# A two-layer encoder on eight cores: the first layer's gates fed from un-normed x, with the norm's factor multiplied onto the sums

## The reference, cut to what matters

```python
def rms_norm(x, g):
    y = xf * lax.rsqrt(jnp.mean(xf * xf, axis=-1, keepdims=True) + EPS)
    return (y * g.astype(jnp.float32)).astype(x.dtype)

# layer 0; x: (2, 8192, 1024)
h = rms_norm(x, norm_0)
z = h @ w_in_0                       # a_u, a_v, a_gate, b_x, b_gate, 1024 columns each
ya = spatial_gating_mixer(a_u, a_v, ...) * jax.nn.silu(a_gate)
yb = multiscale_pool_mixer(b_x, b_group_w_0, b_scale_0) * jax.nn.silu(b_gate)
x = x + jnp.concatenate([ya, yb], axis=-1) @ w_out_0
# layer 1: rms_norm, q/k/v/gate projection, windowed attention, output projection, residual
return rms_norm(x, final_norm)
```

## Time and profile before

| | |
|---|---|
| runs before, median | 768.77 us (768.03 to 769.06) |
| the profiled execution, its own time | 768.59 us |
| its span, slowest core (core 6) | 766.8 us; the eight cores 764.4 to 766.8 us |
| granted TensorE clock, core 6 | 0.988 |
| PE (TensorE matmul) busy | 724.5 us, 94% |
| PEld (weight loads) | 350.2 us, 46% |
| DVE (VectorE), ACT (ScalarE), POOL (GpSimd) | 447.4, 373.5, 184.2 us |
| chain that ended last, by engine | PE 89%, DVE 4%, DMA 3%, issue 2%, ACT 1% |

### The profile page before, as it was taken

How to read it: one execution, slowest core, us unless ns; L and a number is a source line. 1 busy time by engine, 2 the same in 40 slices (tenths; PEclk the granted TensorE clock), 3 DMA queues, 4 the chain that set the end, 5 groups by cost and what they waited for, 6 DMA issues and landing times.

```text
span 766.8 us, 13598 instructions; the slowest of 8 cores (764.4 to 766.8 us)
## 1 busy us (share of the span) xinstructions
PE 724.5 (94%) x4202; PEld 350.2 (46%) x4280; DVE 447.4 (58%) x713; ACT 373.5 (49%) x653; POOL 184.2 (24%) x287
## 2 busy tenths in 40 slices
...
GB/s 167 199 261 60 86 96 96 1 1 1 0 1 1 69 98 83 84 28 93 207 280 127 64 110 32 48 114 60 77 90 84 76 107 81 96 79 86 99 62 83
DMA packets 73477, 66.86 MB, mean 87 GB/s; under 512 B 59440, under 2 KB 59952, under 8 KB 73408
## 3 DMA queue, kind: packets, MB, share of 16 engines
q1 hardware_dynamic: 66144, 43.02, 22.3%
...
## 4 chain that ended last, share of the span: by engine, by line
PE 89%; DVE 4%; DMA 3%; issue 2%; ACT 1%; POOL 0%; DVEq 0%; SPq 0%; POOLq 0%; ACTq 0%
PE ps L151 89%; DVE HT L177 3%; DMA WBG<-wbg 1%; DMA XS<-xa 1%; DMA X<-xb 0%; ACT SQ L157 0%; ACT PTG L157 0%; ACT JUNK L157 0%; DVE SA L166 0%; ACT HT L161 0%; ACT VB L157 0%; DVE PTG L166 0%; ACT TGB L157 0%; DVEq L140 0%; ACT ORAW L161 0%
## 5 line engine op out<-in xcount | busy, mean ns | idle before, releaser
L151 PE MATMUL ps<-HT,WUG 128*128 128x512 bf16 (+1 forms) x624 | 129.3, 357 | 0.8
L157 ACT ACTIVATE PTG<-ps 128x1024 bf16<-128x1024 f32 x96 | 96.6, 1023 | 2.1 <-PE ps L151 2.0
L151 PEld LDWEIGHTS ps<-HT,WUG 128*128 128x128 bf16 x640 | 61.0, 98 | 54.4
L151 PE MATMUL ps<-HT,WBG 128*128 128x512 bf16 (+1 forms) x313 | 72.9, 382 | 6.8 <-DVE HT L177 6.2
L166 DVE TENSOR_TENSOR X<-ps,X 128x512 f32<-128x512 f32 x38 | 26.0, 691 | 88.9 <-PE ps L151 72.5
L157 ACT ACTIVATE JUNK<-X 128x1024 bf16<-128x1024 f32 (+1 forms) x20 | 20.3, 1014 | 104.3 <-DVE X L166 104.2
L151 PE MATMUL ps<-WO0A,YA 128*128 128x512 bf16 x283 | 67.1, 379 | 0.3
L151 PE MATMUL ps<-WO0B,YB 128*128 128x512 bf16 x282 | 67.1, 379 | 0.3
L166 POOL TENSOR_TENSOR M<-M,UC 128x512 f32<-128x512 f32 (+1 forms) x40 | 46.2, 1156 | 82.1 <-DVE M L177 68.1
L151 PE MATMUL ps<-HT,WP 128*128 128x512 bf16 (+1 forms) x314 | 63.6, 359 | 0.3
L173 POOL TENSOR_SCALAR ST<-ST 128x1 f32<-128x1 f32 x53 | 15.3, 288 | 202.3 <-ACT JUNK L157 201.1
...
## 6 DMA issues: line engine op xcount, KB each, us to landing
X<-xp SPq DMA_DIRECT2D x18, 512.0 KB, 8.4
XS<-xa SPq DMA_DIRECT2D x16, 512.0 KB, 7.6
out<-OB SPq DMA_DIRECT2D x15, 512.0 KB, 2.7
WUG<-wug POOLq DMA_DIRECT2D x8, 512.0 KB, 7.3
WBG<-wbg POOLq DMA_DIRECT2D x8, 256.0 KB, 7.8
WXT<-wxt POOLq DMA_DIRECT2D x4, 512.0 KB, 14.9
WV<-wv POOLq DMA_DIRECT2D x4, 512.0 KB, 6.5
WO0A<-wo POOLq DMA_DIRECT2D x4, 512.0 KB, 11.5
```

The lines of the kernel that those rows point to most:

```text
L151: self.op('pe', lambda e: e.matmul(out, lhsT, rhs, start=start, stop=stop), reads, writes, signal)
L157: self.op('act', lambda e: e.activation(out=out, in_=in_, func=func, **kw), reads, writes)
```

## The change

`HR[j]` is a new bf16 tensor: x times `norm_0`, without the norm's factor (`o_raw`, on ScalarE or VectorE). The gates of groups 0 to 3 (`RAW`) take it in place of `HT`. The PSUM bank with the factors is copied to SBUF by ScalarE (`o_keep`, groups 0 to 3), and VectorE multiplies each gate's sums by it in place (`o_post`) before the SiLU. `HT[j]` of these groups is still made, since later stages read it: of group 0 by VectorE after its gates, of group 1 by ScalarE (`o_half`) and GpSimd together during group 2's gates, of groups 2 and 3 by VectorE during group 4's gates. Group 4 keeps the old way.

`load_x(1)` to `load_x(3)` and the small constants are issued right behind `load_x(0)` without waits; `WBG[4]` to `WBG[7]` are issued at W0, `WG`, `WXT` and `WST` at W1, `load_x(4)` at W2. `X0` moves to the region that `WXT` takes later. The loop and `plan` are replaced by one list, `PLAN`: each word has a letter for the step, the group, the block, an engine letter (a ScalarE, d VectorE, p GpSimd, t TensorE) and a PSUM bank. S square, A and U adds, R `o_raw`, C, M, P, D, B the rest of the norm, K `o_keep`, G gate, O `o_post`, L SiLU, T and H making `HT`, F and Y fold and its copy, V `load_wv`.

```diff
-    X0 = region('V').at("X0", [128, 8, 272], F32)
+    X0 = region('WB').at("X0", [128, 8, 272], F32)
...
+    rwc = region('WC')
+    HR1 = rwc.at("HR1", [128, 8, 512], BF16)
+    HR = {1: [HR1], 3: [HR1], 0: [rwc.at("HR0", [128, 8, 256], BF16)],
+          2: [rwc.at("HR2A", [128, 4, 512], BF16), rya.at("HR2B", [128, 4, 512], BF16)]}
+    rl = region('L')
+    RBC = [rl.at(f"RBC{i}", [128, 512], F32) for i in range(2)]
...
+    load_x(1)
+    load_x(2)
+    load_x(3)
+    S.dma('sp', BSC[:], d_bsc[:, :], writes=['bsc'], sem='c_bsc')
+    S.dma('sp', EDGE[:], d_edge[:, :, :], writes=['edge'], sem='c_edge')
+    S.dma('sp', BBC[:], d_bbc[:, :, :], writes=['bbc'], sem='c_bbc')
+    S.dma('sp', GV[:], d_gv[:, :], writes=['gv'], sem='c_gv')
+    S.dma('sp', ESK[:], d_sink[:, :], writes=['esk'], sem='c_esk')
     S.wait_all('pool', ['x0_1'])
     for c in range(4):
         load_wbg(c)
-    load_x(1, 'wbg1')
...
+    RAW = (0, 1, 2, 3)
+
...
+    def o_raw(j, kc, eng, bank):
+        n = GRP[j][2]
+        x, o = xs(j)[:, kc, 0:n], hr(j, kc)
+        if j == 3 and kc not in seen:
+            seen.add(kc)
+            S.alias([f'hr3_{kc}'], [f'hr1_{kc}'])
+        rd, wr = [xkey(j, kc // 2), 'g0'], [f'hr{j}_{kc}']
+        if eng == 'act':
+            S.act(o, x, AF.Copy, rd, wr, scale=G0C[:, kc:kc + 1])
+        else:
+            S.ts('dve', o, x, G0C[:, kc:kc + 1], None, ALU.mult, None, rd, wr)
+
...
+    def o_keep(j, kc, eng, bank):
+        n = GRP[j][1]
+        pr, prk = nrm[j]
+        nrm[j] = (RBC[j % 2], f'rbc{j % 2}')
+        S.copy('act', RBC[j % 2][:, 0:n], pr[:, 0:n], [prk], [f'rbc{j % 2}'])
+
+    def o_half(j, kc, eng, bank):
+        n = GRP[j][1]
+        S.act(TP[kc % 2][:, 0:n], xs(j)[:, kc, :], AF.Copy, [xkey(j, kc // 2), 'g0'], [f'tp{kc % 2}'],
+              scale=G0C[:, kc:kc + 1])
+
+    def o_h(j, kc, eng, bank):
+        n = GRP[j][1]
+        pr, prk = nrm[j]
+        if eng == 'pool':
+            S.tt('pool', HT[j][:, kc, :], TP[kc % 2][:, 0:n], pr[:, 0:n], ALU.mult, [f'tp{kc % 2}', prk], [f'ht{j}_{kc}'])
+        else:
+            S.stt(HT[j][:, kc, :], xs(j)[:, kc, :], G0C[:, kc:kc + 1], pr[:, 0:n], ALU.mult, ALU.mult,
+                  [xkey(j, kc // 2), 'g0', prk], [f'ht{j}_{kc}'])
+
+    def o_gate(j, c, eng, bank):
+        n = GRP[j][2]
+        nrm[j, c] = (PB[bank], f'pb{bank}')
         for kc in range(8):
-            S.mm(pg[:, 0:n], WBG[c][:, kc, :], HT[j][:, kc, 0:n], kc == 0, kc == 7,
-                 [f'ht{j}_{kc}', f'wbg{c}'], [pgk])
-        return lambda: S.act(YB[j][:, c, :], pg[:, 0:n], AF.Silu, [pgk], [f'yb{j}_{c}'])
-
-    def fold(m):
-        for gp in range(2):
-            pw, pwk = next_pb()
-            for gi in range(2):
-                g = 2 * gp + gi
-                for h in range(2):
-                    S.mm(pw[:, gi * 256:gi * 256 + 256], WXT[:, 2 * g + h, m * 128:(m + 1) * 128], WG[:, g, h, :],
-                         h == 0, h == 1, [f'wxt{g}', 'wg'], [pwk], signal=(gi == 1 and h == 1))
-            S.copy('act' if gp else 'dve', WP[:, m, gp * 512:gp * 512 + 512], pw[:, :], [pwk], [f'wp{m}_{gp}'])
+            rhs, rk = (hr(j, kc), f'hr{j}_{kc}') if j in RAW else (HT[j][:, kc, 0:n], f'ht{j}_{kc}')
+            S.mm(PB[bank][:, 0:n], WBG[c][:, kc, :], rhs, kc == 0, kc == 7, [rk, f'wbg{c}'], [f'pb{bank}'])
+
+    def o_post(j, c, eng, bank):
+        n = GRP[j][2]
+        pg, pgk = nrm[j, c]
+        pr, prk = nrm[j]
+        S.tt('dve', pg[:, 0:n], pg[:, 0:n], pr[:, 0:n], ALU.mult, [pgk, prk], [pgk])
+
+    def o_silu(j, c, eng, bank):
+        pg, pgk = nrm[j, c]
+        S.act(YB[j][:, c, :], pg[:, 0:GRP[j][2]], AF.Silu, [pgk], [f'yb{j}_{c}'])
+
...
+    def load_late0(w):
+        if w == 0:
+            for c in range(4, 8):
+                load_wbg(c)
+        elif w == 1:
+            S.alias([f'wxt{h}' for h in range(4)], [f'x0_{h}' for h in range(4)])
+            S.dma('pool', WG[:], d_wg[:, :, :, :], writes=['wg'], sem='c_wg')
+            for h in range(4):
+                S.dma('pool', WXT[:, 2 * h:2 * h + 2, :], d_wxt[h], writes=[f'wxt{h}'], sem=f'wxt{h}')
+            S.dma('pool', WST[:], d_wsT[:, :, :], writes=['wst'], sem='c_wst')
+        elif w == 2:
+            load_x(4)
+        elif w == 3:
+            S.alias([f'wp{m}_{gp}' for m in range(8) for gp in range(2)],
+                    [f'hr{j}_{k}' for j in RAW for k in range(8)])
+
+    PLAN = """
+    R00a0 R01d0 S00a0 R02d0 R03a0 S01a0 R04d0 R05a0 A01p0 S02a0 R06d0 R07a0 S03a0 A02p0 S04a0 S05a0 S06a0 A03p0 A05d0
+    G00t0 R10a0 R11d0 A06p0 S10a0 S07a0 S11a0 A07d0 A11p0 U00d0 C00t1 R12a0 R13d0 S12a0 G01t2 M00d0 S13a0 A12p0 P00p0
+    W0 G02t1 R14a0 R15d0 A13p0 D00d0 S14a0 S15a0 B00t3 A15d0 K00a0 O00d0 O01d0 L00a0 G03t3 O02d0 R16a0 R17d0 L01a0
+    O03d0 G10t0 L02a0 S16a0 L03a0 A16d0 S17a0 G11t1 A17d0 R20a0 R21a0 U10d0 G04t2 S20a0 S21a0 C10t3 O04d0 A21p0 L04a0
+    G12t4 M10d0 R22a0 R23d0 P10p0 S22a0 G05t2 S23a0 A22p0 D10d0 G13t3 O05d0 L05a0 A23p0 R24a0 R25d0 B10t5 S24a0 G06t2
+    S25a0 K10a0 A25d0 G14t5 O06d0 O10d0 L06a0 R26a0 O11d0 G07t2 L10a0 O12d0 L11a0 G15t0 O07d0 L12a0 O13d0 L07a0 O14d0
+    R27a0 G16t1 L13a0 O15d0 L14a0 L15a0 G17t2 O16d0 S26a0 S27a0 A26d0 L16a0 G20t0 O17d0 T10a0 A27p0 H00d0 T11a0 H01d0
+    L17a0 G21t1 H10p0 H02d0 R30a0 U20d0 R31a0 H11p0 H03d0 T12a0 C20t2 H04d0 R32a0 H05d0 G22t3 H12p0 R33a0 M20d0 H06d0
+    T13a0 H07d0 W1 P20p0 R34a0 R35d0 G23t2 R36d0 T14a0 H13p0 R37d0 S30a0 D20d0 S31a0 G24t4 H14p0 S32a0 T15a0 A31p0
+    S33a0 B20t5 T16a0 S34a0 H15p0 K20a0 S35a0 G25t5 O20d0 H16p0 T17a0 A35d0 L20a0 H17p0 W2 O21d0 G26t0 O22d0 L21a0
+    A32p0 O23d0 L22a0 G27t1 O24d0 L23a0 A33p0 O25d0 S36a0 L24a0 O26d0 G30t2 L25a0 A36p0 O27d0 L26a0 L27a0 G31t3 S37a0
+    S40a0 A37d0 S41a0 G32t0 S42a0 U30d0 A41p0 S43a0 C30t1 S44a0 S45a0 A42p0 G33t4 M30d0 A45d0 P30p0 S46a0 G34t1 A46d0
+    A43p0 D30d0 G35t5 S47a0 A47d0 B30t6 U40d0 K30a0 C40t7 O30d0 M40d0 L30a0 O31d0 P40p0 O32d0 G36t2 L31a0 D40d0 L32a0
+    O33d0 B40t0 O34d0 L33a0 G37t3 O35d0 L34a0 O36d0 L35a0 H40d0 L36a0 F00t1 F01t4 O37d0 W3 Y00a0 F10t2 H41d0 Y01a0
+    F11t5 L37a0 F20t1 H42d0 F21t4 Y10a0 F30t3 H43d0 Y11a0 F31t2 Y20a0 F40t6 H44d0 F41t5 Y21a0 F50t1 H45d0 Y30a0 F51t4
+    Y31a0 H46d0 F60t7 F61t3 Y40a0 H47d0 F70t2 Y41a0 F71t6 Y50a0 Y51d0 Y60a0 Y61d0 G40t0 Y70a0 Y71d0 H20d0 G41t1 V0
+    L40a0 H21d0 H22d0 G42t0 H23d0 L41a0 H24d0 G43t1 V1 H25d0 L42a0 H26d0 G44t0 H27d0 L43a0 H30d0 G45t1 V2 H31d0 L44a0
+    H32d0 G46t0 H33d0 L45a0 H34d0 G47t1 V3 H35d0 L46a0 H36d0 H37d0 L47a0
+    """
+    for w in PLAN.split():
+        if w[0] == 'W':
+            load_late0(int(w[1]))
+        elif w[0] == 'V':
+            load_wv(int(w[1]))
+        else:
+            OPS[w[0]](int(w[1]), int(w[2]), ENG[w[3]], int(w[4]))
 ```

More of the change, by code:

```diff
@@ L350, in build @@
         load_wbg(c)
-    load_x(1, 'wbg1')
[L353 to L373, removed]
+    nrm = {}
@@ L375, in blocks, with hr, o_square @@
+    TP = [rv.at(f"TP{i}", [128, 512], F32) for i in range(2)]
+    RAW = (0, 1, 2, 3)
+    def hr(j, kc):
+        t = HR[j]
+        return t[0][:, kc, :] if len(t) == 1 else t[kc // 4][:, kc % 4, :]
     def blocks(n):
         return [(b, min(128, n - 128 * b)) for b in range((n + 127) // 128)]
-    def n_col(j):
-        _, n, _ = GRP[j]
-        sa, sak = SA[j % 2], f'sa{j % 2}'
-        r4, r4k = R4[j % 2], f'r4_{j % 2}'
-        pc, pck = next_pb()
+    def o_square(j, kc, eng, bank):
+        n = GRP[j][1]
+        dst, dk = (SA[j % 2], f'sa{j % 2}') if kc == 0 else (SB, 'sb') if kc == 4 else (SQ[kc % 4], f'sq{kc % 4}')
+        S.act(dst[:, 0:n], xs(j)[:, kc, :], AF.Square, [xkey(j, kc // 2)], [dk])
@@ L383, in n_col, with o_col @@
+    seen = set()
+    def o_col(j, kc, eng, bank):
+        n = GRP[j][1]
+        pc, pck = PB[bank], f'pb{bank}'
+        nrm['c', j] = (pc, pck)
+        sa, sak = SA[j % 2], f'sa{j % 2}'
         for b, m in blocks(n):
```

116 lines of the change are left out of this document (40 added, 76 removed).

## The result

The changed kernel takes 778.94 us (median) and the kernel before 768.47 us: ratio 1.0135 [1.0121, 1.0149], 10.5 us slower. The forecast was 765, 3.7 us faster. The profiled execution took 778.94 us; its slowest core is core 1 (span 777.4), and the eight spans are 773.9 to 777.4.

A forecast was written before the change was run, and what follows sets the result against it. PE bounds the kernel; first-stage changes carry to the end. Group 1's gate G15 at 39 + 59.4 work + 6.1 stall + 1.0 folds + 1.7 clock = 107.2, against 110.9: 768.6 - 3.7 = 764.9, rounded 765; range 755.5 to 771.

The forecast's parts named there:

- G00 can start at 12.5: Start of first stage: first gate, no longer needing the norm, starts at 12.5 us after ScalarE's copies, against 16.5 before.
- if the two queues share the engines evenly: Loads at the start: with even sharing, x1 and WBG 0 to 3 land by 22.3 us, G10 starts at 23.
- rival C: Loads at the start: weights starve behind x; with x taking two thirds, 770.5 us, slower; chance 0.18.
- The bound 8.7 + 8 x 1.76 + 8 x 1.64 = 35.9: Loads: x1, x2 and WBG 0 to 7 have all landed at 35.9 us, which no order of work can pass.
- "HT of group 1 on GpSimd", stall 6.1: Group 2's gates: GpSimd's chain, through ScalarE's T and L, holds G26; 4.2 us plus 1.9 for SBUF meetings, 6.1.
- The port meetings: Group 2's gates: VectorE and GpSimd both reading SBUF take turns; two meetings taken, between none and four, 1.9 us.
- The clock, "I take 1.7": Middle of first stage: stalls around G25 bring another low clock stretch, 1.7 us taken, between none and 3.4.
- Small durations: First stage: ScalarE copies 0.6 us (0.62 for 512 columns), VectorE's R 0.48 or less, multiplies O 0.69.
- The folds: Folds of first stage: 11 copies, 6.6 us against 7.0 of PE with latencies between; 1.0 us taken (0 to 2).
- The last quarter of x4: Loads: x4 is requested quarter by quarter at 47 to 61 us and lands by 68, before S46; nothing waits.
- If x takes all: Extreme case of rival C: WBG0 lands and the first gate starts at 31.5 us; 783 us.
- Making HT of groups 2 and 3 beside group 4's gates: Group 4's gates: 12.0 us of VectorE beside 13.8 us of gates, costing nothing; without that cover at most 1 us.

The follow-up runs named there:

- Experiments 6 and 7: experiment 5 with group 0's norm finished before x1 is touched; 6, x1 to x3 requested at once: 784.61 us; 7, loads held as in kernel before: 776.57 us.
- 4: The kernel before with x1 and x2 requested right behind x0, without their waits; 770.44 us, 1.0028 to the kernel before.
- 9: experiment 3 with x1 to x3 requested only once x0 has landed; 775.64 us, 1.0093 to the kernel before.
- Experiment 10: experiment 3 with x1 requested at once, x2 and x3 only when WBG3 has landed; 775.34 us, 1.0089 to the kernel before.
- experiment 3: The changed kernel with group 1's HT made by VectorE alone, no ScalarE T words or GpSimd products; 772.1 us, 1.0053 to the kernel before.
- experiment 2: The changed kernel with x1 held behind WBG1, x2 behind WBG5, x3 behind half of x2; 787.71 us, 1.025 to the kernel before.
- Experiment 1: The changed kernel with GpSimd's block 3 product of group 1's HT waiting for VectorE's group 2 diagonals; 775.04 us, 1.0085 to the kernel before.
- experiment 5: experiment 3 with GpSimd's power for group 2 moved ahead of W1's issues; 773.32 us, 1.0055 to the kernel before.

## Why the prediction was wrong

**The first gate, "G00 can start at 12.5".** Its copies were ready; its weights were not. The step that failed is the sharing of the engines: "if the two queues share the engines evenly" holds from 12 us on (53.9 to 50.4%) but not before. SyncE's transfers are issued from 1 us on, those of x0 and x1 before GpSimd's first at 6.8, and from 8 to 12 us GpSimd's get 2.9% of the engines. This is rival C's direction, with a chance of 0.18, and it passed the point from which I let it decide: WBG7 at 42.0 (41), G15 at 43.9 (42.7). Its shape was another: C had x take a fixed larger part all along, and here x takes nearly all for 4 us and half afterwards. Experiments 6 and 7 show the price of the early requests with the list held fixed (8.0 us), 4 in the old kernel (1.9 us), and 9 shows that the order of filling decides. The Trainium skill ("DMA: Bandwidth & Descriptors", section "Queues, rings and completion order") has each engine take turns between the queues packet by packet; the windows from 12 us on agree (165 packets against 203 and 169), the window before doesn't (7 against 294). I had called WBG's descriptors being as long as x's an argument against C; by the rows of 12:16 a packet of q0 is 1.9 KB and one of q1 3.6 KB. The 5.7 us of G0C, a 4 KB transfer beside x0, was the better witness. What the 4 us consist of, a backlog inside the engines or late descriptors, no run here tells apart.

A second thing was wrong in the same step. The bound 8.7 + 8 x 1.76 + 8 x 1.64 = 35.9 left out x3, whose four transfers are requested right behind x2's. With them it is 8.7 + 12 x 1.76 + 8 x 1.64 = 42.9, and the last of the twenty landed at 43.6. Experiment 10, with x2 and x3 held back, has WBG7 at 36.9.

The late start alone would have stayed inside the range: with G15 at 43.9 and every other term as predicted, the stage ends at 112.1, which is 769.8. What carried the time out of it is the next two steps.

**"HT of group 1 on GpSimd", stall 6.1.** The source was right and the mechanism and the place were not. I had a chain of T, H and L that would hold G26. PE waits for no L and no bank there; the wait comes two steps earlier, at B20, for a diagonal on VectorE. The port meetings, which I had priced at 1.9 us on top, are nearly all of it: D20 alone loses 5.9. I counted a meeting as a pair of instructions in which the second waits once, from the one pair at the kernel's end. There VectorE was first and GpSimd waited. Here GpSimd is first, and when its product is done the next is already there. The Trainium skill ("SBUF — State Buffer", section "Who interferes with whom") has the first to issue keep the shared pair for the whole instruction and the other fully blocked. The trace agrees for a single one (1.69 us, experiment 3). For a row it shows both outcomes: D20 waited for all five here and in experiment 2 (6.55 us both times), and the operations before it, from 50.45 us, got their turn after each product. What decides between the two is open. Experiment 1 gives back 3.9 us by order alone, and 3 gives back 6.8 by taking the products off GpSimd.

**The clock, "I take 1.7".** It is 7.3. The terms of a stall and of its clock aren't independent: here each of the three longer waits has gates at the low level behind it. Against the full rate they lose 1.7 us from 57.3 on (behind the wait of 2.8), 3.9 from 69.0 to 78 (behind that of 5.5; 1.87 and 1.91 us for four matmuls of 512 that take 1.03 later), and 1.7 from 94.65 on (behind that of 1.66). The length of the wait alone doesn't decide it: in experiments 1 and 3 the same last wait, 1.65 us, is followed by a gate at full rate. Experiment 3, with 3.5 us at B20, still has 0.93 over 60:112. I took 1.7 from a single stretch, 42:46, as if there could be only one.

**Small durations.** ScalarE's HR of 512 columns took 0.71 us and TP 0.72 (I took 0.62, that of a square); VectorE's HR 0.42 where nothing met it, below the 0.48 taken. The multiplies O took 0.69, as taken. The folds cost nothing that shows. The last quarter of x4 landed at 80.0, not by 68, since it was asked for at 73.0; PE didn't wait for it here, but in experiment 5 it did.

**A rival's sum.** "If x takes all" ends in 783. By the prediction's own terms G15 at 53.5 gives 53.5 + 59.4 + 6.1 + 1.0 + 1.7 = 121.7, hence 779.4. That this is the measured time is luck: WBG0 landed at 17.9 and not at 31.5.

**What was right.** PE's work is unchanged: with 59.4 us after G15, the waits and the slow gates add up to the stage's end. Making HT of groups 2 and 3 beside group 4's gates costs nothing: PE runs 13.98 us through them and on into WP without a wait. The stages behind moved and didn't change (656.0 against 655.9). R26 and x2 were ready before WBG7, so the list's tie of L10 to x2 didn't bind.

So of the 14.2 us between the forecast's 107.2 and 121.4, 4.9 are the start, 4.7 the waits in the middle (with another place and cause), and 4.6 the clock less what I had put on the folds. Why the best form, experiment 3, still loses 2.8 to 5.4 us to the kernel before stays partly open: its first gate starts 1 us later, and its D20 waits for the power behind W1; but the attempts to mend either (5, 7, 9, 10) each found the next word of the list in the way. No version here beat the kernel before; whether some other list would is not shown.
